# First attention: the next head's keys in two halves, a step apart between the engines, and the first sweep's V products one step later

## What is computed

```
keys   = w_uk[h] @ c_kv.T                     # 64 x 1024, c_kv is the latent (1024 x 128)
scores = q[h] @ keys, scaled, + bias, masked  # by blocks of 128 queries, causal
p      = softmax(scores)                      # each row
att[h] = p @ (c_kv @ w_uv[h].T)               # V of the head
```

## Time and profile before

| | |
|---|---|
| median of 3 executions | 3510.32 us (3502.98 to 3512.49) |
| profiled execution, its own time | 3510.73 us |
| its span in the trace | 3509.0 us |
| busy share of the span: PE, PEld, DVE, ACT, POOL | 92%, 70%, 52%, 28%, 26% |
| mean granted TensorE clock | 0.956 |
| first attention's units | from about 669 us to about 1062 us |
| in 686.21 to 1026.70 us (14 heads): PE, DVE, ACT busy | 271.85, 236.00, 208.58 of 340.49 us |

### The profile page before, as it was taken

How to read it: one execution, slowest core, us unless ns; L and a number is a source line. 1 busy time by engine, 2 the same in 40 slices (tenths; PEclk the granted TensorE clock), 3 DMA queues, 4 the chain that set the end, 5 groups by cost and what they waited for, 6 DMA issues and landing times.

```text
span 3509.0 us, 36793 instructions
## 1 busy us (share of the span) xinstructions
PE 3242.2 (92%) x14026; PEld 2462.4 (70%) x14026; DVE 1841.2 (52%) x3008; ACT 969.7 (28%) x1810; POOL 900.7 (26%) x566
## 2 busy tenths in 40 slices
PE   7999999877789998989999999998998999799988
PEld 3577788555557886668887788887867887465457
DVE  1499993467664447871331544444233416766661
ACT  2320111366651003560101100001213212655450
POOL 0133233000002324653332433332233342200002
PEclk9999999999999999999999999999999899898799
DMA  8012233100001111112332111112111110000011
GB/s 211 13 45 66 90 99 96 72 18 7 19 19 49 50 35 43 37 54 97 98 136 87 41 49 48 48 48 102 60 55 62 60 48 27 1 1 13 0 58 75
DMA packets 185861, 196.37 MB, mean 56 GB/s; under 512 B 12257, under 2 KB 152029, under 8 KB 184029
## 3 DMA queue, kind: packets, MB, share of 16 engines
q1 hardware_dynamic: 170669, 142.08, 13.7%
q10 hardware_dynamic: 15024, 51.98, 4.0%
HBM read 153.15 MB, written 40.89 MB: 55 GB/s over the span
## 4 chain that ended last, share of the span: by engine, by line
PE 68%; DVE 10%; issue 9%; POOL 4%; ACT 4%; DMA 2%; DVEq 2%; ACTq 1%; POOLq 1%; SPq 0%
PE psum L629 65%; DVE arena L1689 3%; PE psum L633 3%; DVE rounded L1689 2%; DVE arena L1692 2%; DVE arena L1846 2%; POOL stat L1174 1%; POOL arena L1228 1%; ACT arena L1300 1%; DMA arena<-z_d 1%; POOL rounded L1185 1%; DVE arena L1834 1%; POOL arena L1245 1%; ACTq L1306 0%; DVEq L1842 0%
## 5 line engine op out<-in xcount | busy, mean ns | idle before, releaser
L629 PE MATMUL psum<-rounded,rounded 128*128 128x512 f32 (+2 forms) x9504 | 2214.7, 393 | 106.4 <-DVE rounded L1689 84.8
L629 PEld LDWEIGHTS psum<-rounded,rounded 128*128 128x128 f32 x9504 | 1799.5, 190 | 514.0 <-issue 95.9
L629 PE MATMUL psum<-arena 128*128 128x512 f32 (+15 forms) x2450 | 779.0, 487 | 56.8 <-ACT arena L1300 40.7
L1183 POOL CAST rounded<-arena 128x1024 fp32r<-128x1024 f32 (+1 forms) x190 | 206.4, 1087 | 1717.8 <-DMA arena<-in_w_in 815.4
L629 PEld LDWEIGHTS psum<-arena 128*128 128x128 f32 (+4 forms) x2450 | 399.7, 202 | 321.0 <-issue 277.8
L1300 ACT ACTIVATE arena<-psum 128x512 f32<-128x512 f32 (+9 forms) x572 | 310.1, 568 | 863.0 <-PE psum L629 711.8
L1185 POOL TENSOR_TENSOR rounded<-arena,rounded 128x1024 fp32r<-128x1024 f32 (+1 forms) x190 | 465.3, 2449 | 28.2 <-issue 1.3
L633 PE MATMUL psum<-ident,arena 128*128 128x128 f32 (+1 forms) x1816 | 284.7, 301 | 86.6 <-DVE arena L1689 30.3
L633 PEld LDWEIGHTS psum<-ident,arena 128*128 128x128 f32 (+1 forms) x1816 | 234.1, 154 | 156.9 <-issue 51.6
L1689 DVE TENSOR_TENSOR arena<-arena,psum 128x512 f32<-128x512 f32 (+1 forms) x176 | 125.8, 733 | 354.9 <-PE psum L629 335.3
L1689 DVE TENSOR_TENSOR rounded<-arena,rounded 128x1024 fp32r<-128x1024 f32 (+1 forms) x132 | 198.6, 1536 | 210.0 <-ACT rounded L1303 209.4
(11 more groups left out here) (137 smaller groups left out, 1487.4 us busy)
## 6 DMA issues: line engine op xcount, KB each, us to landing
arena<-in_w_in SPq DMA_DIRECT2D x84, 512.0 KB, 3.7
arena<-in_w_ffn_up SPq DMA_DIRECT2D x44, 512.0 KB, 3.8
arena<-in_w_ffn_down SPq DMA_DIRECT2D x22, 512.0 KB, 3.6
z_d<-arena ACTq DMA_DIRECT2D x32, 256.0 KB, 3.0
gate_d<-arena ACTq DMA_DIRECT2D x16, 512.0 KB, 3.8
arena<-in_w_ssm_out SPq DMA_DIRECT2D x16, 512.0 KB, 4.2
arena<-z_d SPq DMA_DIRECT2D x8, 1024.0 KB, 4.8
arena<-gate_d ACTq DMA_DIRECT2D x16, 512.0 KB, 3.5
```

The lines of the kernel that those rows point to most:

```text
L629: return pe.matmul(out, lhsT, rhs, start=start, stop=stop)
L1183: pool.tensor_copy(high_part, raw)
```

## The change

Three things change, all in the first attention.

1. Keys: `keys_twice(h, half)` projects 512 columns into one bank. Half 0 of the next head comes in step 0, half 1 in step 2 (`keys_at1`), each behind that step's scores and ahead of the transposes. ScalarE rounds a half one step later (`key_highs`, steps 1 and 3), VectorE subtracts two steps later (`key_lows`, steps 2 and 4) and frees its bank. The query rows are rounded on ScalarE in step 2 (`query_highs`) and subtracted on VectorE in step 5 (`query_lows`).
2. The first sweep's products with V come in steps 1 and 2 instead of 0 and 1. The second sweep stays.
3. VectorE's low part of `hT` comes two steps later than before; ScalarE's high part stays.

```diff
-        summing_at1 = {n + PV_LAG1 + m: (n, 2 * m) for n in sweeps1 for m in range(units1[n]["nk"] // 2)}
+        summing_at1 = {n + PV_LAG1 + (units1[n]["nk"] == 4) + m: (n, 2 * m) for n in sweeps1
+                       for m in range(units1[n]["nk"] // 2)}
...
-        stacked_at1 = {TT * h + 2: h + 1 for h in range(HEADS - 1)}
+        keys_at1 = {TT * h + 2 * m: (h + 1, m) for h in range(HEADS - 1) for m in range(2)}
+        queries_at1 = {TT * h + 2: h + 1 for h in range(HEADS - 1)}
...
-            def keys_twice(h):
-
-                out = bank(("kk", h), 2, FOR_SCORES)
-                pe.wait_ge(*vacated(("kk", h)))
-                pe.wait_ge(*vacated(("kk", h), 1))
+            def keys_twice(h, half):
+
+                name = ("kk", h, half)
+                out = bank(name, 1, FOR_SCORES)
+                pe.wait_ge(*vacated(name))
                 pe.wait_ge(uk_doubled, h + 1)
-                for lo, hi in chunks(S):
-                    last = mm(out[:, lo:hi], uk_twice[h % 2], ckvT[:, lo:hi])
-                last.then_inc(full(("kk", h)), 1)
+                mm(out, uk_twice[h % 2], ckvT[:, half * 512:half * 512 + 512]).then_inc(full(name), 1)
...
             for s in range(STEPS1):
-                if s in stacked_at1:
-                    keys_twice(stacked_at1[s])
                 if s < N1:
...
+                if s in keys_at1:
+                    keys_twice(*keys_at1[s])
                 if s in turned_at1:
...
-            def stack_highs(h):
+            def key_highs(h, half):
+
+                act.wait_ge(*completed(("kk", h, half)))
+                act.activation(kshi[h % 2][:, half * 512:half * 512 + 512], psum_of(("kk", h, half)),
+                               ACT.Copy).then_inc(key_high[half], 1)
+
+            def query_highs(h):
 
                 r, j = 64 * (h % 2), h // 2
-                act.wait_ge(*completed(("kk", h)))
-                act.activation(kshi[h % 2], psum_of(("kk", h)), ACT.Copy)
-                act.activation(qstack[h % 2][r:r + 64, :], qT[r:r + 64, j, :], ACT.Copy).then_inc(stack_high, 1)
+                act.activation(qstack[h % 2][r:r + 64, :], qT[r:r + 64, j, :], ACT.Copy).then_inc(query_high, 1)
...
-                if s in stacked_at1:
-                    stack_highs(stacked_at1[s])
+                if s - 1 in keys_at1:
+                    key_highs(*keys_at1[s - 1])
+                if s in queries_at1:
+                    query_highs(queries_at1[s])
...
-            def stack_lows(h):
+            def key_lows(h, half):
+
+                here = slice(half * 512, half * 512 + 512)
+                dve.wait_ge(key_high[half], h + 1)
+                tt_(kslo[h % 2][:, here], psum_of(("kk", h, half)), kshi[h % 2][:, here].bitcast(F32),
+                    ALU.subtract).then_inc(empty(("kk", h, half)), 1)
+
+            def query_lows(h):
...
-                dve.wait_ge(stack_high, h + 1)
-                tt_(kslo[h % 2], psum_of(("kk", h)), kshi[h % 2].bitcast(F32), ALU.subtract).then_inc(empty(("kk", h)), 1)
+                dve.wait_ge(query_high, h + 1)
...
-                if s in stacked_at1:
-                    stack_lows(stacked_at1[s])
-                if s in split_at1:
-                    k = split_at1[s]
+                if s - 2 in keys_at1:
+                    key_lows(*keys_at1[s - 2])
+                if s - 3 in queries_at1:
+                    query_lows(queries_at1[s - 3])
+                if s - 2 in split_at1:
+                    k = split_at1[s - 2]
```

More of the change, by code:

```diff
@@ L359, in hybrid_two_blocks @@
         maximum4 = sem("maximum4")
-        stack_high = sem("stack_high")
+        key_high = [sem(f"key_high{m}") for m in range(2)]
+        query_high = sem("query_high")
         stack_ready = sem("stack_ready")
@@ L793, in _ @@
             pe.wait_ge(phase_done, 4 * 1)
-            def keys_twice(h):
-                out = bank(("kk", h), 2, FOR_SCORES)
-                pe.wait_ge(*vacated(("kk", h)))
-                pe.wait_ge(*vacated(("kk", h), 1))
+            def keys_twice(h, half):
+                name = ("kk", h, half)
+                out = bank(name, 1, FOR_SCORES)
+                pe.wait_ge(*vacated(name))
                 pe.wait_ge(uk_doubled, h + 1)
-                for lo, hi in chunks(S):
-                    last = mm(out[:, lo:hi], uk_twice[h % 2], ckvT[:, lo:hi])
-                last.then_inc(full(("kk", h)), 1)
-            keys_twice(0)
+                mm(out, uk_twice[h % 2], ckvT[:, half * 512:half * 512 + 512]).then_inc(full(name), 1)
+            for half in range(2):
+                keys_twice(0, half)
             for tt in range(TT):
@@ L1211, in _ @@
                 if h >= 2:
-                    pool.wait_ge(*completed(("kk", h - 2)))
+                    pool.wait_ge(*completed(("kk", h - 2, 1)))
                 pool.tensor_copy(uk_twice[h % 2].rearrange("p (a b) -> p a b", b=HD),
@@ L1393, in _ @@
             act.wait_ge(phase_done, 4 * 1)
-            def stack_highs(h):
+            def key_highs(h, half):
[3 more added lines that the diff above has]
+            def query_highs(h):
                 r, j = 64 * (h % 2), h // 2
-                act.wait_ge(*completed(("kk", h)))
-                act.activation(kshi[h % 2], psum_of(("kk", h)), ACT.Copy)
-                act.activation(qstack[h % 2][r:r + 64, :], qT[r:r + 64, j, :], ACT.Copy).then_inc(stack_high, 1)
-            stack_highs(0)
+                act.activation(qstack[h % 2][r:r + 64, :], qT[r:r + 64, j, :], ACT.Copy).then_inc(query_high, 1)
+            for half in range(2):
+                key_highs(0, half)
+            query_highs(0)
             for s in range(STEPS1):
@@ L1813, in stack_lows @@
                 q_high = qstack[h % 2][r:r + 64, :].bitcast(F32)
-                dve.wait_ge(stack_high, h + 1)
-                tt_(kslo[h % 2], psum_of(("kk", h)), kshi[h % 2].bitcast(F32), ALU.subtract).then_inc(empty(("kk", h)), 1)
+                dve.wait_ge(query_high, h + 1)
                 tt_(qstack[h % 2][other:other + 64, :], qT[r:r + 64, j, :], q_high, ALU.subtract).then_inc(stack_ready, 1)
-            stack_lows(0)
+            for half in range(2):
+                key_lows(0, half)
+            query_lows(0)
             for tt in range(TT):
```

## The result

The changed kernel takes 3456.28 us (median of 5 runs, 3455.89 to 3456.79), the kernel before 3510.32 us (5 runs on the same chip, 3502.98 to 3514.24). The ratio is 0.9848 with an interval of 0.9834 to 0.9861: 54 us are given back, where 37.7 were forecast. Ratios are of fast runs alone: in the batch of the last experiments one run of the kernel before took 5455.23 us at a granted clock of 0.553 and is left out.

The account below looks back on a forecast made before the run. No engine is full; heads 1 to 14 of the first attention, 340.5 us, are a loop of waits. Less 297.8 for the new heads and 5 for the clock, 37.7 come back: 3510.7 - 37.7 = 3473 us, range 3450 to 3496.

Parts of the forecast that it names:

- The two waits: TensorE's waits in a head: 2.24 us at step 0's first V product, 2.59 us at step 4's scores.
- the walk: One head followed step by step after the change, from step 7's 1024-wide mask; 297.8 us for the 14 heads.
- the term of the even heads: Six heads with a part of `hT`: VectorE's 1.2 us in step 3 makes the half's bank late; 21.5 us each.
- The first two heads: Head 1, with no copy of bank 7 at its start, 20.2 us; head 2, without DMA issue or `hT`, 20.8 us.
- The clock: Slow stretches cost the 14 heads about 10 us; half, 5 us, was taken to remain after the change.
- The fixed cost of the cut: Two halves instead of one cost 0.16 us more on VectorE and 0.15 us more on ScalarE.
- The ends of the stage: Start and end of the first attention, and its last head: nothing counted as gained or lost.
- Only the start gains: Rival: ScalarE's hand-overs cost 0.1 to 0.2 us more each or the half's bank comes late; heads 22.7, 3490 us; chance 0.20.
- All waits go: Rival: every head falls to TensorE's own 19.6 us, giving back 66 us, 3445 us; chance 0.12.
- The loop is not shortened: Rival: the second sweep starts at 14 as before, since step 3's copies come no earlier; 3508 us; chance 0.08.
- The slower one: Rival: step 5's scores wait for the second half, 3.4 us later than reckoned or more; 3526 us at 3.8; chance 0.05.

Follow-up runs that it names:

- The parts alone: Kernel before with only the first sweep's V products a step later, 3493.07 us; changed kernel with those products back in steps 0 and 1, 3468.32 us.
- the whole keys: Changed kernel with keys in one 1024-column piece, TensorE in step 0, ScalarE in step 1, VectorE in step 2: 3459.54 us.
- the halves: Changed kernel with both key halves and the queries in step 2 on all three engines: 3486.59 us.
- the three edits: Changed kernel with transposes copied ahead of the sweep's copy, 3456.58 us; queries in steps 5 and 6, 3471.9; keys' second half a step earlier, 3456.82.

## Why the prediction was right, and where its sizes were off

**The mechanism was right.** The two waits that the walk took away are gone, the wait for ScalarE moved to step 1's transposes (forecast about 2 us, measured 1.73), VectorE waits at step 2's scores (forecast about 2, measured 1.27), and the second sweep starts 11.86 us into the head, forecast 12.3. The parts alone (7.5 and 38.9 us in the heads) show both halves of the argument, and the whole keys and the halves together show that more hangs on the steps between the engines than on the cut. What the prediction didn't price by itself is the place of `hT`: it is worth 15 of the 54 us, and the prediction only had VectorE's wait of 10.7 us for it.

**The walk** gave 297.8 us for the 14 heads, measured 291.86. Of the 5.9 us, 3.8 are the term of the even heads: 21.5 for heads with `hT`, measured 20.86 to 20.88. I had VectorE's 1.22 us push the half's bank late. It does, and the weight load of step 5's scores waits for it, but by less, and the head doesn't show it. In an even head of the changed kernel (its t = 0 is 787.85):
```profile
800.61 0.69 DVE L1699 TENSOR_TENSOR rounded<-psum,rounded 128x512 fp32r<-128x512 f32 x1
...
801.34 0.76 PEld L632 LDWEIGHTS psum<-rounded,rounded 128*128 128x128 f32 x4 [0.62 <-DVE rounded L1699]
801.35 0.85 PE L632 MATMUL psum<-rounded,rounded 128*128 128x512 f32 x3
```
The scores start at 13.50, 0.05 behind the end of the subtraction, and in the odd head at 13.27, 0.26 behind it; yet the even head is the shorter one, 20.88 for 20.95. Another 1.7 are the odd heads, 20.95 for 21.3 but for one of 21.31: from the start of the first V product to step 2's scores it was 1.22 us, not 1.5, from there to the half of the keys 0.64, not 0.75, and from step 2's copies to the second sweep 4.01, not 4.15. The first two heads make up the rest, 0.4.

**The clock** was mis-sized by 5 us. I left half of 10; the 14 heads have none of it left, their granted clock is 1.00 where it was 0.95. The kernel before with more products gives 6.7 us of the heads back, with three of its heads still 1.5 us and more above 23.61, so the 10 of the prediction was about right as a whole, and only the half that was to stay was wrong.

By the Trainium skill, "TensorE: Matmul & The Clock Gate", Part 1, the throttled clock is the default and activity releases it; as the prediction read it, the 5 us go too. For the changed kernel that reading gave the better number. The V products alone speak against it as a rule for less waiting: their clock went down, from 0.95 to 0.93. What decides it is not the length of one wait. There the waits are 2.3 us at most and 13 of 14 heads are slowed, while this head of before (805.17 to 828.79) ran at a granted clock of 1.00:
```profile
808.30 1.74 PE L629 MATMUL psum<-arena 128*128 128x512 f32 x4 [2.47 <-ACT arena L1300]
...
818.50 0.87 PE L629 MATMUL psum<-rounded,rounded 128*128 128x512 f32 x4 [2.73 <-DVE rounded L1689]
```
That the long heads are the clock's is shown. Work in the wait took the slow stretch out of most heads of before, gave one to head 6, and in the last head of the changed kernel moved it behind the head. Which stretch falls, and why, stays open; so it is not shown either that the change's full clock comes from its shorter waits.

**The fixed cost of the cut** was as counted. The group of the halves in the changed kernel (count, busy us, mean ns, idle before; answers to the earlier trace rows):
```profile
L1699 DVE TENSOR_TENSOR rounded<-psum,rounded 128x512 fp32r<-128x512 f32 x28 | 19.2, 686 | 0.3 <-ACT rounded L1400 0.3
```
Two halves are 1.37 us against 1.225. The 0.15 us a head fall into VectorE's waits, of which 30.5 us are left. The section of the Trainium skill that the prediction names for this, in "VectorE: DVE Perf Modes", on the fixed extra latency per instruction, advises tiles of at least 512 elements. The halves are 512 wide, so that advice doesn't speak against them as the prediction had it.

**The ends of the stage** were counted as nothing. The last head costs 1.66 us more, for a wait that the kernel of before did not have there, with the slow stretch behind it. What follows its mask costs 2.31 less; its clock was 0.90 before (in the window 1045.50 to 1062.74) and is 1.00. The 5.1 us further out are no gain of the change that is shown; as much comes without it: in the kernel before with two products more per head the first mask is 1.4 us earlier and the later stages, from the last copy of `attT`, are 3.8 us shorter (2442.2 against 2446.0 us; 2442.9 in the changed kernel). Over all the kernels of this study the first mask lies between 680.78 and 686.28 us and the later stages take 2437.1 to 2446.5. What moves them was not tried. A sum that stops at the attention's end gives 49.3 us.

So 37.7 + 5.9 + 5 - 1.7 + 2.3 + 5.1 = 54.3. Of the 17 us by which the time lies below the forecast, 5.1 are drift that has nothing to do with the change. That the two ends of the stage, which the prediction left out, nearly cancel is luck: with two products more in the last head the slow stretch went from the one to the other.

**The rivals.** "Only the start gains" (3490) needed hand-overs of 0.1 to 0.2 us more each; they were shorter. "All waits go" (3445) fell: 35.9 us of waits for ScalarE stay, and the three edits that each took one away found the next. Its floor of 19.6 us a head was also too high, as the 340.49 us it was worked out from hold TensorE's slow stretches: by the same working the changed kernel has (291.86 - 35.9) / 14 = 18.3. "The loop is not shortened" fell with the second sweep at 11.86. The slower one would have needed the half's bank 3.4 us late; with its rounding 0.7 us late a head lost 0.1 to 0.2 us.

## What to carry to other kernels

When three engines hand one piece of work along within one step of a loop, give each its own step first, and cut the piece second: here the 14 heads lost 34.5 us without the steps and 7.5 without the cut. Read such a gain from the loop itself: parts of the program that nobody edited differed by up to 9 us between traces, the same heads, in the one pair there is, by 0.03. Work may be put into a wait only where the wait is; the 1.2 us of the queries were free in step 5 and cost 0.6 to 1.8 us a head in step 6, the slow stretches behind them included. And a wait of TensorE costs more than its length where a slow stretch follows it, so read the granted clock by head, before and after, and in the last turn of the loop too.

## What the runs showed that was not expected

Adding work to TensorE made a stage faster: 28 products more, with PE busy for 14.9 us more, took the 14 heads from 340.49 to 333.76 us, and the whole from 3512.05 to 3497.74 (medians); about half of that lies outside these heads. Two products more took the last head from 20.46 to 18.82 us, and the stretch behind it from 15.19 to 16.87. Less waiting did not always raise the clock: with the V products moved alone TensorE's two main waits fell from 65.9 to 55.6 us and the granted clock from 0.95 to 0.93. And an edit elsewhere in the loop can set it: with the queries in step 6 the odd heads ran at 0.92 and took 22.73 us, the even ones at 1.00 and 21.50.
